# Encoder layer on one core: Fourier mixer first, a transform over half the tokens, group scales apart, top eights on half rows

## What is computed

```python
def token_mixer(h, w_in, conv_w, g_sgu, w_sp, b_sp, g_grp, w_out):
    z = h @ w_in
    zb, zc, za, zf, zu, zv = jnp.split(z, SPLITS, axis=-1)
    ya = rms_norm(short_conv_mixer(zb, zc, za, conv_w), g_grp[:CONV_W])                # 384 channels
    yf = rms_norm(fourier_mixer(zf), g_grp[CONV_W:CONV_W + FOURIER_W])                 # 256 channels
    yc = rms_norm(spatial_gating_mixer(zu, zv, g_sgu, w_sp, b_sp), g_grp[CONV_W + FOURIER_W:])  # 384
    return jnp.concatenate([ya, yf, yc], axis=-1) @ w_out

def fourier_mixer(zf):   # per head of 64 channels: real part of a 2D transform, over tokens and channels
    f = zf.reshape(b, s, FOURIER_GROUPS, HEAD_DIM)
    return jnp.real(jnp.fft.fft2(f, axes=(1, 3), norm='ortho'))

# encoder: h = modulate(x); x = x + gate * token_mixer(h); h = modulate(x); x = x + gate * moe(h); rms_norm(x)
# moe: aff = softmax(h @ w_router) over 16 experts; each expert takes its top 2 n / 16 tokens
#      (128 of the prompt, 64 of the sample), gated MLP of 1024, times its affinity, added back
```

## Time and profile before

| | us |
|---|---|
| median of 3 runs | 1622.46 (1622.09 to 1623.38) |
| the profiled execution | 1621.7 |
| its span, first to last instruction | 1619.9 |
| PE busy | 1472.7 (91%) |
| DVE busy | 1064.8 (66%) |
| ACT busy | 771.7 (48%) |
| mean granted clock | 0.953 |

### The profile page before, as it was taken

One profiled execution on the slowest core, in us unless ns is written; L12 is line 12 of the kernel. 1 busy time (PEld: TensorE's weight loads), 2 busy tenths in 40 slices (PEclk: granted clock), 3 DMA queues, 4 the chain that ended last, 5 costly groups with the idle time before them and its releaser, 6 DMA issues.

```text
span 1619.9 us, 22647 instructions
## 1 busy us (share of the span) xinstructions
PE 1472.7 (91%) x8583; PEld 1289.8 (80%) x8583; DVE 1064.8 (66%) x1443; ACT 771.7 (48%) x1006; POOL 166.8 (10%) x128
## 2 busy tenths in 40 slices
PE   2999998889989877289999999999999999999993
PEld 1877776468778755189999999999999999999992
DVE  3522133646768956767777777777777777777776
ACT  4311122412433131246666666666666566666664
POOL 2000000000000000001121011111201210211120
PEclk9999999889999977689999999999999999999996
DMA  9234433445332043178788778877877887888786
GB/s 328 83 117 136 138 117 119 143 156 201 98 117 72 20 170 142 39 234 247 255 250 268 240 243 272 245 263 243 268 236 255 263 257 249 246 264 239 266 272 249
DMA packets 218804, 324.82 MB, mean 201 GB/s; under 512 B 7548, under 2 KB 174536, under 8 KB 218760
## 3 DMA queue, kind: packets, MB, share of 16 engines
q1 hardware_dynamic: 209624, 297.32, 55.3%
q0 software_dynamic: 8064, 26.30, 7.0%
q10 hardware_dynamic: 1072, 0.59, 0.1%
HBM read 292.69 MB, written 31.49 MB: 200 GB/s over the span
## 4 chain that ended last, share of the span: by engine, by line
PE 76%; DVE 11%; issue 4%; ACT 4%; DMA 3%; SPq 2%; POOL 0%; POOLq 0%; DVEq 0%; ACTq 0%
PE ps L1445 23%; PE ps L1135 21%; PE ps L1443 10%; PE ps L1466 3%; PE ps L1458 3%; PE ps L1467 3%; PE ps L1459 3%; PE ps L1462 3%; PE ps L1448 1%; DVE aff L1829 1%; DVE vals L1826 1%; DMA gffn_b<-in_g_ffn 1%; DVE idxu L1828 1%; PE ps L1434 1%; DVE wlo L1927 1%
## 5 line engine op out<-in xcount | busy, mean ns | idle before, releaser
L1445 PE MATMUL ps<-xT,whi 128*128 128x384 f32 x2048 | 576.3, 356 | 1.3 <-DVE xT L1933 1.3
L1927 DVE TENSOR_TENSOR wlo<-raw,whi 128x2048 fp32r<-128x2048 f32 x192 | 437.4, 2293 | 192.0 <-ACT whi L1041 192.0
L1443 PE MATMUL ps<-xT,wlo 128*128 128x192 f32 x1792 | 455.2, 254 | 0.0
L1445 PEld LDWEIGHTS ps<-xT,whi 128*128 128x128 f32 x2048 | 367.9, 189 | 2.2 <-issue 1.6
L1041 ACT ACTIVATE whi<-raw 128x2048 fp32r<-128x2048 f32 x192 | 362.2, 1906 | 0.0
L1443 PEld LDWEIGHTS ps<-xT,wlo 128*128 128x128 f32 x1792 | 342.4, 191 | 0.0
L1135 PE MATMUL ps<-hT,wring 128*128 128x512 f32 x1224 | 294.4, 399 | 5.9 <-DVE hT L1572 5.9
L1135 PEld LDWEIGHTS ps<-hT,wring 128*128 128x128 f32 x1224 | 231.6, 191 | 60.0 <-DVE hT L1572 6.4
L1135 PE MATMUL ps<-wo,Yhl 128*128 128x512 f32 x576 | 147.6, 418 | 20.8 <-DVE x L1757 9.4
L1135 PEld LDWEIGHTS ps<-wo,Yhl 128*128 128x128 f32 x576 | 116.0, 204 | 48.4 <-issue 21.9
L1071 ACT ACTIVATE gu_l<-ps 128x384 f32<-128x384 f32 x128 | 62.9, 491 | 155.8 <-PE ps L1445 155.8
(11 more groups left out here) (207 smaller groups left out, 1607.2 us busy)
## 6 DMA issues: line engine op xcount, KB each, us to landing
raw<-in_w_gate SPq DMA_DIRECT2D x64, 1024.0 KB, 5.0
raw<-in_w_up SPq DMA_DIRECT2D x64, 1024.0 KB
raw<-in_w_down SPq DMA_DIRECT2D x64, 1024.0 KB, 5.4
wraw<-in_w_in SPq DMA_DIRECT2D x34, 512.0 KB, 6.1
wraw<-in_w_ada SPq DMA_DIRECT2D x32, 512.0 KB, 4.8
ada_w<-in_w_ada SPq DMA_DIRECT2D x16, 512.0 KB, 9.1
acc_d<-x SPq DMA_DIRECT2D x12, 512.0 KB, 2.7
h_d<-h SPq DMA_DIRECT2D x12, 512.0 KB, 3.9
```

What stands on the lines that cost most here:

```text
L1443: pe.matmul(out[:, 0:CAP], wlo[:, slot, w], xT[:, k, 0:CAP], start=False, stop=False, skip_group_check=True)
L1445: mm = pe.matmul(out[:, 0:2 * CAP], whi[:, slot, w], xT[:, k, :], start=k == 0, stop=k == KB - 1, skip_group_check=True)
L1927: dve.tensor_tensor(wlo[:, j % SPL, :], raw[:, j % RAW, :], whi[:, j % SPL, :].bitcast(F32), ALU.subtract).then_inc(w_split, 1)
```

## The change

- **Order.** FIRST is now zf0, zf1. After them: zv0, ab, zv1, vt0, zv2, vt1, zu0, vt2, zu1, zu2, zc0, sv (gating), za0, zb0, zc1, za1, ssq of the gating group, zb1, zc2, za2, zb2. The w_ada products follow every block from the second, two each.
- **Transform.** The tokens n and n + s/2 are first added (for the even frequencies) and subtracted (for the odd ones): `ab` is made for both halves of the tokens, ACT copies the first, DVE adds and subtracts the second. The constants then cover half the tokens and a quarter of the frequencies a matmul: 4 loads for the prompt in place of 8, 2 for the sample in place of 4, matmuls of 256 columns and 128 in place of 512 and 256. Results are written in steps of two.
- **Weights.** wo6 and wo7 are loaded within the blocks (after zb1 and zc2), wo5 between the constants, wo0 to wo4 after them.
- **Scales.** NORMS = (2, 0, 1). Each group has its own ssq job, root and reciprocal: gating within the blocks, convolution after the transform, Fourier after the first w_out tile. gtm_b and shf_b are broadcast after the second of these, x and gffn_b after the splits and squares, gsf_b after the third; DVE makes gsf_b behind tile 0's x2.
- **Top eights.** The rows are laid as two halves, on partitions 0 to 15 and 32 to 47 (48 partitions are worked on). As many rounds as before, 16 and 8, on rows of 512 and 256; then a merge: the second half's list reversed, compared with the first, the larger of each pair kept. The prompt's rounds are spread over steps 11 to 22 of the sample's blocks, none in the residual; its lists are transposed at tile 1.
- The router's work for the prompt's last tiles moves between other blocks (ROUTER).

```diff
-SOFTMAX_STEP, AFF_STEP = 5, 6
-ROUNDS_LATE = 2
-NORMS = (0, 2, 1)
+IDX_TILE = 1
+HALF_AT = 32
+NORMS = (2, 0, 1)
+ROUTER = {2: (("tokens", 5), ("blocks", 6)), 3: (("logits", 6),), 4: (("tokens", 6), ("blocks", 7)), 6: (("logits", 7),),
+          8: (("tokens", 7),)}
+SOFTMAX_STEP, AFF_STEP = 8, 10
+ROUNDS = {11: 2, 12: 2, 14: 1, 15: 2, 16: 2, 17: 1, 19: 2, 20: 2, 21: 1, 22: 1}
+FIRST = (("zf", 0), ("zf", 1))
+WO_AHEAD = {("zb", 1): 6, ("zc", 2): 7}
...
+    order = ["zf0", "zf1", "zv0", "ab0", "zv1", "vt0", "zv2", "vt1", "zu0", "vt2", "zu1", "zu2", "zc0", "sv0", "za0", "zb0",
+             "zc1", "za1", "ssq2", "zb1", "zc2", "za2", "zb2"]
...
+                if s == 0 and (kind, i) in WO_AHEAD:
+                    out.append(("wo", WO_AHEAD[kind, i]))
         if s == 0:
-            for m in range(TL[0]):
-                out += [("wo", m), ("dft", 0, m)]
+            out += [("dft", 0, 0), ("dft", 0, 1), ("wo", 5), ("dft", 0, 2), ("dft", 0, 3)]
+            out += [("wo", b) for b in (0, 1, 2, 3, 4)]
...
+    def split_may_go(c, ahead):
+        if ahead[0] == "wo":
+            return raw_n[ahead] <= raw_n[c] + 1
+        early = ring_n[ahead] < ring_n[c] + SR and ahead[1] == c[1]
+        return early and all(x[0] != "ada" for x in stream[raw_n[c]:raw_n[ahead] - RS + 1])
...
-                wait_filled(sp, "ssq", s)
+                wait_filled(sp, "ssq", s, 0)
+                for col, dst, arrived in ((2 * D, gtm_b, gtm_in), (3 * D, shf_b, ffn_in)):
+                    sp.dma_start(dst[:, :], mod_d[s:s + 1, col:col + D].to_broadcast([P, D])).then_inc(arrived, 16)
                 sp.wait_ge(y_lo, KB * (s + 1))
+                sp.wait_ge(sq_done, KB * (s + 1))
                 load_xr(T0[s])
                 load_xr(T0[s] + 1)
                 sp.dma_start(gffn_b[:, :], a["g_ffn"].to_broadcast([P, D])).then_inc(ffn_in, 16)
+                wait_filled(sp, "ssq", s, 1)
+                sp.dma_start(gsf_b[:, :], mod_d[s:s + 1, 4 * D:5 * D].to_broadcast([P, D])).then_inc(ffn_in, 16)
...
                 for par, name in enumerate(("even", "odd")):
                     out = [open_bank(name, s, fb) for fb in range(2)]
+                    for c in range(chunks * par, chunks * (par + 1)):
+                        n = raw_n["dft", s, c]
+                        wait_drained(pe, "ab", s, c, 1)
                         pe.wait_ge(ws_in[n % RS], 16 * (n // RS + 1))
                         for fb in range(2):
+                            for q in range(2):
+                                for ab in range(2):
+                                    at_col = half * q + quarter * ab
+                                    ins = mm(out[fb][:, quarter * q:quarter * (q + 1)], AB[s][:, c, q, fb, ab, :],
+                                             wraw[:, n % RS, at_col:at_col + quarter], first and q == ab == 0, last and ab == 1)
...
             def topk_eight(s, n):
-                eight, row = slice(8 * n, 8 * n + 8), aff[0:NE, 0:W[s]]
+                eight, row = slice(8 * n, 8 * n + 8), aff[0:HALF_AT + NE, 0:W[s] // 2]
...
             def topk_end(s):
+                step(dve.tensor_copy(other, vals[second, 0:cap][:, ::-1]))
+                step(dve.tensor_scalar(where, idxu[second, 0:cap][:, ::-1], float(W[s] // 2), None, ALU.add))
+                step(dve.tensor_copy(i0, idxu[first, 0:cap]))
+                step(dve.tensor_tensor(merge_m[first, 0:cap], v0, other, ALU.is_ge))
+                step(dve.tensor_tensor(i0, i0, where, ALU.subtract))
+                step(dve.tensor_tensor(v0, v0, other, ALU.max))
+                step(dve.tensor_tensor(i0, i0, merge_m[first, 0:cap], ALU.mult))
+                ins = dve.tensor_tensor(i0, i0, where, ALU.add)
```

More of the change, by code:

```diff
@@ L170, in bank_events @@
                     filled(kind, s, i, g)
[L171 to L176, removed]
+            for what, t in ROUTER.get(n, ()) if s else ():
+                if what == "tokens":
+                    job("lt", 0, t)
+                if what == "blocks":
+                    router_blocks(0, t)
+                if what == "logits":
+                    job("lg", 0, t)
             if s and n == AFF_STEP:
@@ L460, in encoder_kernel @@
     first_s = min(n for n, c in enumerate(ring) if c[1] == 1)
-    dft_n = {c: n for n, c in enumerate(c for c in stream if c[0] == "dft" and (c[2] + 1) % (TL[c[1]] // 2))}
+    parity_of = {c: 4 * c[2] // TL[c[1]] for c in stream if c[0] == "dft"}
+    dft_n = {c: n for n, c in enumerate(c for c in stream if c[0] == "dft" and (c[2] + 1) % (TL[c[1]] // 4))}
+    splits = list(split_n)
     ws_in = [sem(f"ws_in{i}") for i in range(RS)]
@@ L1255, in mixers, with square_sums @@
+                    for what, t in ROUTER.get(n, ()) if s else ():
+                        if what == "tokens":
+                            router_tokens(0, t)
+                        if what == "blocks":
+                            router_blocks(0, t)
+                        if what == "logits":
+                            router_logits(0, t)
                     if s and n == AFF_STEP:
                         affinity_rows(0)
+            def square_sums(s, k):
+                pe.wait_ge(sq_added, 5 * s + {2: 2, 0: 4, 1: 5}[k])
+                pe.wait_ge(ones_set, 1)
+                out = open_bank("ssq", s, k)
+                for t in range(TL[s]):
+                    ins = pe.matmul(out[:, t:t + 1], SQ[k][s][:, P * t:P * (t + 1)], ones[:, :], start=True, stop=True)
+                fill(ins, "ssq", s, k)
@@ L1519, in split_lo, with split_ahead, split_next @@
                                   ALU.subtract).then_inc(ws_lo, 1)
-            def split_ahead(chunks):
-                last = ring_n[chunks[-1]] + SR - 1
-                end = len(ring) if ring_n[chunks[0]] >= first_s else first_s
-                while n_split[0] <= min(last, end - 1) and loads_without(chunks[0], ring[n_split[0]]):
-                    split_lo(ring[n_split[0]])
+            def split_ahead(c):
+                while n_split[0] < len(splits) and split_may_go(c, splits[n_split[0]]):
+                    split_lo(splits[n_split[0]])
+                    n_split[0] += 1
+            def split_next(n=1):
+                for _ in range(n):
+                    split_lo(splits[n_split[0]])
                     n_split[0] += 1
@@ L1829, in topk_eight @@
[L1829 removed]
+                step(dve.max_index(idxu[0:HALF_AT + NE, eight], vals[0:HALF_AT + NE, eight], row))
+                step(dve.match_replace(row, vals[0:HALF_AT + NE, eight], row, -2.0))
             def topk_end(s):
+                cap = CAPS[s]
+                first, second = slice(0, NE), slice(HALF_AT, HALF_AT + NE)
+                v0, i0, other, where = vals[first, 0:cap], idxf[first, 0:cap], merge_v[first, 0:cap], merge_i[first, 0:cap]
```

527 lines of the change are left out of this document (278 added, 249 removed).

## The result

The changed kernel takes 1546.67 us (median of 4, 1545.11 to 1547.93) against 1622.28 of the kernel before beside it: a ratio of 0.9535, 95% interval 0.9519 to 0.9552. The forecast was 1549.5, the range 1534 to 1572. Its profiled execution took 1547.9 with a span of 1545.9; before, 1621.7 and 1619.9.

What follows compares the result with a forecast made beforehand. The prediction saw PE busy in the experts and prompt blocks, with waits and low clock at the joints as the soft part. Stage terms summed to -73.0 us, giving 1548.7, or 1549.5 at the median; range 1534 to 1572.

Steps and rivals of the forecast that it cites:

- Prompt blocks: Prompt's w_in blocks: w_ada wait gone (-3.2), gating (+5.4), sums (+1.9) and load delays (+1) added; +5.1 us.
- That rival: Prompt's blocks: the two w_out loads stall them, each by 4 us, giving 1557; chance 0.08.
- T to the third tile: From PE's last prompt block and w_ada products (T) to the third w_out tile: 85.5 us becomes 49.5, -36.0.
- Sample blocks: Sample's blocks: waits for v and h2T and most low clock behind them go; 107.2 us becomes 97.5, -9.7.
- The estimate for DVE: Last 12 steps of the sample's blocks: DVE has 62 us against PE's 59.6, ending 4 to 5 late.
- The sample's joint: End of the sample's mixers and two tiles: DVE sets the pace, tile 2 starts at 39.5; -12.0 us.
- Tiles 3 and 4: Sample's last tiles and router: waits for the prompt's list and h2T go; 41.1 us becomes 25.7, -15.4.
- the list: Sample's list before the experts: 8 rounds on 256-long rows, less merging and a second copy; -5.0 us.
- Clock low in the joints: Joints: PE stays at 1.2 GHz throughout, costing about +33 us, 1583; chance 0.10.
- DVE setting the sample's end: Sample's end: DVE's operations cost 15% more, so tile 0 and all after slide by 10 us, 1560; chance 0.10.
- Half rows not cheaper: Top eights: a round costs by partitions too, putting DVE 25 us behind, 1580; chance 0.04.
- The experts' clock: Expert stage: PE rests less before it, clock may fall; at 0.88 the kernel takes 1654 us; chance 0.03.

Runs made afterwards that it cites:

- e10: Changed kernel with the loads of wo6 and wo7 behind the transform's constants instead of among the prompt's last blocks: 1550.62 us.
- e9: Changed kernel with the transform back over all tokens (8 and 4 loads of constants), the new order kept: 1558.93 us.
- e11: Changed kernel with gsf_b made by DVE before it scales tile 0's banks, instead of after tile 0's x2: 1555.09 us.
- e12: Changed kernel with the three group scales held until the last sums are there, after tile 0: 1551.40 us.
- e1: Changed kernel with weight tiles split two ahead instead of three during the sample's first three blocks: 1538.09 us.
- e3: Changed kernel with the prompt's last two top-eight rounds and merge moved from the sample's blocks to behind the convolution group's scale: 1540.54 us.
- e7: Changed kernel with the top eights back on full rows of 1024 and 512 on 16 partitions, no merge, rounds in their new places: 1574.31 us.
- e8: Changed kernel with the prompt's third and fourth loads of transform constants held back, so that PE waits for each: 1553.91 us.
- e2: Changed kernel with the transform's recombination and the Fourier splits put before wo2's split at the end of the prompt's mixers: 1544.91 us.
- e5: Kernel before with only the transform over half the tokens added, the order of blocks untouched: 1617.31 us.
- e4: Changed kernel with splits two ahead, recombination before wo2's split, and the last two rounds and merge moved, all three together: 1529.49 us.

## Why the prediction was right

The time was right to 3 us. Eight of the nine stages are within 3 us of the forecast; the ninth missed by 5.7, which the others, 6.7 better in sum, made good. That the total came so close is in part luck. Step by step:

- **Prompt blocks**, +5.1, measured +4.1. The two w_out loads cost nothing (I took 1); e10 shows it from the other side. That rival is out.
- **T to the third tile**, -36.0, measured -39.0. The transform ended at T+15.7 (T+15.8 forecast). Tile 0's last 12 matmuls began at T+29.4 (T+30), behind a wait of 3.06 for a w_out split. The third tile came at T+46.6 for 49.5, because gsf_b landed 5.5 us after its issue where I took 6.5, and tile 1 ran at the high clock; the terms of my sum gave h2 at T+47.3, which I had rounded up to 48. e9, e11, e12 and e10 give the pieces: 13.0, 5.6, 3.7, 2.4, together 24.7 of the 39.0, if what they cost one by one adds up (no run takes them out together), each read from one execution of a stage that varies by 2.6 without an edit. Another 7.3 is work that only moved (gating, 5.4, and a third of the sums, 1.9) and shows up again in the blocks. The last 7 were not tried apart.
- **Sample blocks**, -9.7, measured -4.0: the failed step. I wrote that "the 4.2 for h2T" go, "the logits now have the head products between the transposes and themselves", and that "splits run two blocks ahead". They run three ahead, and the split of a tile whose load had just been issued stands before the drain of h2T. The wait became 5.39 with 2 us of low clock behind it; e1 shows it, -7.8, and the stage would have been -11.8. I had asked what PE has to do in the meantime and not what the draining engine has queued ahead of the drain. The estimate for DVE held: 62 us against 59.6 of PE, 4 to 5 us late; it was 5.1.
- **The sample's joint**, -12.0, measured -14.5. The mechanism was right (DVE sets it: e3, and e9's transform hidden to 0.01 us), the start of tile 0 was at +11.6 for +12; the last sums ended at +25.9 for +26. Over-sized is what follows: h2 at +34.9 for +38, since gsf_b landed in 4.2 us and DVE did not wait for it at all.
- **Tiles 3 and 4**, -15.4, measured -16.4, and **the list**, -5.0 both: a round of 256 takes 0.42, 0.41, 0.40 for its three parts as worked out, and e7 gives back 4.8 of it.
- **The rivals.** Clock low in the joints: 1583 was wrong, since there was one wait between the prompt's chunks, of 1.03. e8 makes two of over 3 us and loses 10.1 in that joint, 5.6 of it the waits themselves; the rival's terms for it were 12.7 and 7 of low clock. Waits between the sample's chunks were not tried. DVE setting the sample's end by 10 us more: no, it was the 5 us reckoned. Half rows not cheaper: e7. The experts' clock: 0.98, and 1.5 us more than before, which no run here explains. Whether the order of the splits sets PE's wait for w_out stays open as well, since e2 is within the noise.

The parts do not add: alone on the kernel before, transform and half rows gave 3 and 20 us; taken out of the changed one, they cost 12 and 28. As e5 and e9 show it, a shorter transform is worth its columns only where the splits, the scales and the broadcasts behind it are short too, and where DVE of the next stage comes along.

## What to carry to other kernels

Before crediting a wait as gone, write out the queue of the engine that must end it, in its own order, and look for a split or copy ahead of it whose load has just been issued: letting an engine prepare tiles further ahead can make a drain later. Work that must be done by an engine at a joint (rounds, merges) belongs in the first place behind the joint where that engine waits for another anyway; such a move and one less tile ahead gave 6 and 9 us here, and with the move of e2 17. And test a part in both kernels, since a part that gives nothing alone may be what the rest lives on.

## What the hardware showed that was not expected

- What the low clock costs behind a wait hardly grows with the wait. Behind waits of 22.13, 6.12, 2.78 and 2.02 us at the same place (e7, after, e9, e4) the 8 sums and tile 0 took 15.1, 15.4, 15.4 and 13.8, against 12.1 at the high level (0.95 + 11.18). It can fail to come at all: behind 2.04 us tile 1 of the sample took 11.16 in e12.
- It need not begin at once: behind the same wait of 3.06 us the 12 Fourier matmuls took 4.58 in after and 2.97 in e3, where the tile after them, behind a further wait of 0.42, took 12.63 instead of 11.17.
- A broadcast of 512 KB issued 8.7 and 3.3 us behind the load before it landed in 4.2 and 5.5 us; before, with two broadcasts issued within 1 us ahead of it, it took 8.0.
